# Gating and squares moved into a scan, diagonal matmuls for scaled transposes, and a first modulation in two halves

## The reference

```python
mod = silu(cond) @ w_mod + b_mod                      # six rows of 1024, two conditionings
h = rmsnorm(x + pos, norm1_w) * (1 + sc1) + sh1       # pos: a 2-D grid of sines, latent tokens only
gate_a, gate_b, u, v, z, xbc, dt_f, dt_b = split(h @ w_in)
y_f, h_f = ssd_chunked(xh, dt_f, ...)                 # 32 heads of 64, chunks of 128 tokens, state 128
y_r, h_b = ssd_chunked(flipped, ...)
y = y_f + flip(y_r) + xh * d_skip                     # 640 x 2048
y = group_rmsnorm(y * silu(z), ssd_norm_w, 4 groups)  # mean of squares over 512 columns
merged = sigmoid(gate_a) * (y_a @ w_branch_a) + sigmoid(gate_b) * (y @ w_branch_b)
x = x + g1 * (merged @ w_out)                         # then a routed mixture of experts
```

## Time and profile before

| | us |
|---|---|
| median of 3 runs | 1561.56 (1560.65 to 1561.61) |
| the profiled execution | 1557.0 |
| its span, first to last instruction | 1555.3 |

### The profile page before, as it was taken

How to read it: one execution, slowest core, us unless ns; L and a number is a source line. 1 busy time by engine, 2 the same in 40 slices (tenths; PEclk the granted TensorE clock), 3 DMA queues, 4 the chain that set the end, 5 groups by cost and what they waited for, 6 DMA issues and landing times. The chain is left out here.

```text
span 1555.3 us, 20614 instructions
## 1 busy us (share of the span) xinstructions
PE 1302.7 (84%) x7887; PEld 1154.1 (74%) x7887; DVE 835.1 (54%) x972; ACT 668.5 (43%) x1031; POOL 263.5 (17%) x285
## 2 busy tenths in 40 slices
PE   3999989799998999947788844999880799999970
PEld 1789989799997888944566643999770688888860
DVE  2411442277665111105778759333464499999966
ACT  2423330144443222127567737111140477777743
POOL 0600000000000010025599861000002000000002
PEclk9999999999999999978899966999985899999995
DMA  9992112112212243154466541331645599999935
GB/s 385 412 363 71 66 38 99 37 55 82 70 67 82 90 148 123 52 185 142 149 190 196 199 153 78 115 107 64 259 162 194 195 397 405 421 403 413 413 154 203
DMA packets 62497, 289.09 MB, mean 186 GB/s; under 512 B 9104, under 2 KB 13648, under 8 KB 42064
## 3 DMA queue, kind: packets, MB, share of 16 engines
q1 hardware_dynamic: 49424, 242.19, 42.0%
q0 software_dynamic: 12608, 45.62, 7.5%
q10 hardware_dynamic: 384, 0.16, 0.0%
HBM read 239.51 MB, written 48.43 MB: 185 GB/s over the span
## 5 line engine op out<-in xcount | busy, mean ns | idle before, releaser
L212 PE MATMUL banks<-rounded,rounded 128*128 128x320 f32 (+1 forms) x1168 | 366.1, 313 | 20.2 <-DVE rounded L735 6.9
L213 PE MATMUL banks<-rounded,rounded 128*128 128x320 f32 (+1 forms) x1168 | 363.9, 312 | 0.0
L214 PE MATMUL banks<-rounded,rounded 128*128 128x320 f32 (+1 forms) x1168 | 363.7, 311 | 0.0
L191 DVE TENSOR_TENSOR rounded<-words,rounded 128x2048 fp32r<-128x2048 f32 x52 | 119.2, 2292 | 225.7 <-ACT rounded L183 223.4
L1916 DVE TENSOR_TENSOR rounded<-words,rounded 128x2048 fp32r<-128x2048 f32 x96 | 219.7, 2290 | 32.9 <-ACT rounded L1907 32.0
L212 PEld LDWEIGHTS banks<-rounded,rounded 128*128 128x128 f32 (+1 forms) x1168 | 220.8, 189 | 21.5 <-issue 13.9
L213 PEld LDWEIGHTS banks<-rounded,rounded 128*128 128x128 f32 (+1 forms) x1168 | 220.9, 189 | 0.3
L214 PEld LDWEIGHTS banks<-rounded,rounded 128*128 128x128 f32 (+1 forms) x1168 | 220.6, 189 | 0.3
L1907 ACT ACTIVATE rounded<-words 128x2048 fp32r<-128x2048 f32 x96 | 183.9, 1916 | 47.1 <-PE banks L2032 39.4
L183 ACT ACTIVATE rounded<-words 128x2048 fp32r<-128x2048 f32 x52 | 99.3, 1909 | 138.0 <-PE banks L233 62.8
L1191 ACT ACTIVATE words<-words,words 128x128 f32<-128x128 f32 x320 | 97.7, 388 | 62.0 <-DMA words<-decay_sums 62.0
(11 more groups left out here) (269 smaller groups left out, 1971.7 us busy)
## 6 DMA issues: line engine op xcount, KB each, us to landing
words<-in_units SPq DMA_DIRECT2D x52, 1024.0 KB, 5.0
words<-in_wg SPq DMA_DIRECT2D x32, 1024.0 KB, 7.4
words<-in_wu SPq DMA_DIRECT2D x32, 1024.0 KB, 7.7
words<-in_wd SPq DMA_DIRECT2D x32, 1024.0 KB, 8.2
words<-decay_sums SPq DMA_DIRECT2D x40, 512.0 KB, 3.8
words<-in_w_mod_rest SPq DMA_DIRECT2D x32, 512.0 KB, 4.3
slot_rows<-words POOLq DMA_DIRECT2D x27, 512.0 KB, 24.1
expert_rows<-words POOLq DMA_DIRECT2D x25, 512.0 KB, 9.1
```

Of the source, the lines that this page charges most:

```text
L191: self.nc.vector.tensor_tensor(self.lo[:, i % 2, :], self.raw[:, i % 2, :], self.hi[:, i % 2, :].bitcast(F32), ALU.subtract).then_inc(self ...
L212: nc.tensor.matmul(out, lhs[0](k), rhs[0](k), start=(k == 0), stop=False)
L213: nc.tensor.matmul(out, lhs[0](k), rhs[1](k), start=False, stop=False)
L214: last = nc.tensor.matmul(out, lhs[1](k), rhs[0](k), start=False, stop=(k == nk - 1))
```

## The change

Three things are done, and a number of small ones follow from them.

- **First modulation in two halves.** The weight pieces 0 and 2 (first half of shift and of scale) are loaded first, then weight unit 0, then pieces 1 and 3, then unit 1. Two small vectors move ahead of x. The sums and columns of the first half (three of now six `s_cols`) release the first four slices; the second half's products stand in TensorE's list between the second and third tile, its sums after the third tile. The position table becomes a row table and a column table, spread by the transfer. A root on an unused element is done at the start. The zeros, the constants and the further weight units wait for the sixth `s_cols`.
- **Gating, squares and roots in the scan.** For 18 of the 20 (chunk, group) pairs, SP loads silu(z) (256 KB, one slot), GpSimd multiplies (`apply_z`, at even sub-steps), ScalarE squares (`squares`, at odd sub-steps from 7) into the same slot. Mean, reciprocal and root of the first 16 are done at the scan's end.
- **Diagonal transposes.** In the normalization GpSimd writes `ident` times the reciprocal root as a diagonal for each pair, and TensorE multiplies the block of y with it, in place of a scaling and a transpose. ScalarE and VectorE split 512 elements at once. The norm weight goes onto the weight units of branch b: GpSimd scales each of eight units (`scale`) before it is split.

The diff, cut to what matters:

```diff
+O_SQ = O_TMP + 4192
+O_NW = O_K + 848
+GROUPS = [(c, g) for c in (0, 4, 3, 2, 1) for g in range(G)]
+GATED, ROOTED = 18, 16
...
+    def scale(self, pool, i, column):
         i += self.first
-        act.wait_ge(self.raw_loaded[i % 2], 16 * (i // 2 + 1))
+        pool.wait_ge(self.raw_loaded[i % 2], 16 * (i // 2 + 1))
+        v = self.raw[:, i % 2, :].rearrange("p (k n) -> p k n", k=KI)
+        self.nc.gpsimd.tensor_tensor(v, v, column.unsqueeze(2).broadcast_to([P, KI, UNIT // KI]),
+                                     ALU.mult).then_inc(self.scaled, 1)
+    def split_hi(self, act, i, scaled=False):
+        i += self.first
+        if scaled:
+            act.wait_ge(self.scaled, i + 1)
+        else:
+            act.wait_ge(self.raw_loaded[i % 2], 16 * (i // 2 + 1))
...
-    WM = [kit.at(o, 4096) for o in (O_H, O_H + 5120, O_MG, O_BC + 2304)]
-    RB = (4, 5, 7, 3)
+    WM = [kit.at(o, 4096) for o in (O_H, O_MG, O_H + 5120, O_BC + 2304)]
+    RB, SB = (4, 0, 7, 1), ((6, 0), (2, 384))
     x = kit.at(O_X, NC, D)
-    pos = kit.at(O_X + 5120, NC - 1, D)
+    pos_row, pos_col = kit.at(O_X + 5120, NC - 1, 512), kit.at(O_X + 7168, 512)
...
-            sp.dma_start(x, io["x"].rearrange("(c p) d -> p c d", p=P)).then_inc(s_x, 16)
-            sp.dma_start(pos, io["pos"].rearrange("(c p) d -> p c d", p=P)).then_inc(s_pos, 16)
-            sp.dma_start(kit.at(O_K, KOFF["end"]), io["consts"]).then_inc(s_k, 16)
             sp.dma_start(n1, io["norm1"]).then_inc(s_small, 16)
             sp.dma_start(bcol, io["b_mod_cols"].rearrange("p (q k) -> p q k", q=2)).then_inc(s_small, 16)
-            for j in range(4):
+            sp.dma_start(x, io["x"].rearrange("(c p) d -> p c d", p=P)).then_inc(s_x, 16)
+            sp.dma_start(pos_col, io["pos_col"]).then_inc(s_pos, 16)
+            for h in range(2):
+                sp.dma_start(pos_row[64 * h:64 * h + 64].rearrange("p c d -> p (c d)"),
+                             io["pos_row"][h:h + 1].partition_broadcast(64)).then_inc(s_pos, 16)
+            sp.dma_start(kit.at(O_K, KOFF["end"]), io["consts"]).then_inc(s_k, 16)
+            for j in (0, 2):
                 sp.dma_start(WM[j], io["w_mod"][j]).then_inc(s_w[j], 16)
             w.load(sp, 0)
+            for j in (1, 3):
+                sp.dma_start(WM[j], io["w_mod"][j]).then_inc(s_w[j], 16)
             w.load(sp, 1)
-            sp.wait_ge(s_dve, 2)
+            sp.wait_ge(s_dve, 4)
             sp.dma_start(scr["xp"].rearrange("(c p) d -> p c d", p=P), x).then_inc(s_xp, 16)
-            sp.wait_ge(s_sum, 1)
-            sp.wait_ge(s_cols, 3)
+            sp.wait_ge(s_sum, 2)
+            sp.wait_ge(s_cols, 6)
...
-            pool.wait_ge(s_cols, 3)
+            pool.wait_ge(s_cols, 6)
...
+            def modulate(half):
+                for j in (half, 2 + half):
+                    pe.wait_ge(s_w[j], 16)
+                    for k in range(KD):
+                        g = k % 4
+                        last = nc.tensor.matmul(ps[32 * g:32 * g + 32, RB[j], :], sc[:, k, :], WM[j][:, k * 512:(k + 1) * 512],
+                                                start=(k < 4), stop=(k >= 4))
+                    last.then_inc(s_row, 1)
+            def add_parts(half):
+                bank, at = SB[half]
+                for n, j in enumerate((half, 2 + half)):
+                    pe.wait_ge(s_part, 2 * half + n + 1)
+                    for q in range(4 * j, 4 * j + 4):
+                        last = nc.tensor.matmul(ps[:, bank, at + 2 * q:at + 2 * q + 2], row[:, q * P:(q + 1) * P], sel, start=True, stop=True)
+                last.then_inc(s_sum, 1)
...
+            modulate(0)
+            add_parts(0)
+            pe.wait_ge(s_dve, 6 + NC)
...
+                if k in (0, 4):
                     turn(k // 2 + 1)
+                if k == 1:
+                    pe.wait_ge(s_full, 8)
+                    modulate(1)
+                if k == 2:
+                    add_parts(1)
+                    pe.wait_ge(s_cols, 6)
+                    turn(2)
...
+            nc.scalar.activation(unused, sc[:, 0, 31:32], ACT.Sqrt).then_inc(s_table, 1)
...
+            copy_rows(0)
             w.split_hi(act, 0)
             for k in range(KD):
+                if k == 4:
+                    copy_rows(1)
+                    w.split_hi(act, 1)
...
+            columns(0)
             w.split_lo(dve, 0)
             for k in range(KD):
+                if k == 4:
+                    columns(1)
+                    w.split_lo(dve, 1)
...
+            def load_z(i):
+                if i:
+                    sp.wait_ge(squared, i)
+                c, g = GROUPS[i]
+                sp.dma_start(Z, scr["z"][c * P:(c + 1) * P, cols(g)]).then_inc(z_loaded, 16)
...
+                if j >= 3 and j % 2 and (j - 1) // 2 < GATED:
+                    load_z((j - 1) // 2)
...
+            def apply_z(i):
+                c, g = GROUPS[i]
+                if c:
+                    pool.wait_ge(y_whole, 2 * i + 2 - N0)
+                else:
+                    pool.wait_ge(y_steps, 2 * i + 2)
+                pool.wait_ge(z_loaded, 16 * (i + 1))
+                nc.gpsimd.tensor_tensor(X[:, c, cols(g)], X[:, c, cols(g)], Z, ALU.mult).then_inc(z_applied, 1)
...
+                if j and j % 2 == 0 and j // 2 <= GATED:
+                    apply_z(j // 2 - 1)
...
+            def squares(i):
+                c, g = GROUPS[i]
+                act.wait_ge(z_applied, i + 1)
+                nc.scalar.activation(Z, X[:, c, cols(g)], ACT.Square, accum_out=ssq[:, i:i + 1]).then_inc(squared, 1)
             for j, (c, g, q) in enumerate(subs):
+                if j >= 7 and j % 2:
+                    squares((j - 7) // 2)
...
+            squares(GATED - 1)
+            act.wait_ge(mean_done, 2)
+            nc.scalar.activation(rr[:, 0:ROOTED], rr[:, 0:ROOTED], ACT.Sqrt).then_inc(root_done, 1)
...
+            dve.wait_ge(squared, ROOTED)
+            nc.vector.tensor_scalar(ssq[:, 0:ROOTED], ssq[:, 0:ROOTED], 1.0 / GW, EPS, ALU.mult, ALU.add).then_inc(mean_done, 1)
+            dve.wait_ge(mean_done, 1)
+            nc.vector.reciprocal(rr[:, 0:ROOTED], ssq[:, 0:ROOTED]).then_inc(mean_done, 1)
...
+    early, late = kit.at(O_TMP + 2560, 12, P), kit.at(O_NW + KI, 8, P)
+    diag = lambda i: early[:, i, :] if i < 12 else late[:, i - 12, :]
...
+            for i in range(GATED, n):
+                c, g = GROUPS[i]
+                sp.dma_start(Z[:, i - GATED, :], scr["z"][tokens(c), cols(g)]).then_inc(s_z[i - GATED], 16)
+            sp.dma_start(nw, io["ssd_nw"]).then_inc(s_in, 16)
...
+            def scales(i):
+                nc.gpsimd.tensor_tensor(diag(i), ident, rr[:, i:i + 1].broadcast_to([P, P]), ALU.mult).then_inc(s_diag, 1)
+            for i in range(ROOTED):
+                scales(i)
+            for i in range(GATED, n):
+                c, g = GROUPS[i]
+                pool.wait_ge(s_z[i - GATED], 16)
+                nc.gpsimd.tensor_tensor(X[:, c, cols(g)], X[:, c, cols(g)], Z[:, i - GATED, :], ALU.mult).then_inc(s_y, 1)
+            pool.wait_ge(s_in, 16)
+            w.scale(pool, 0, nw)
+            pool.wait_ge(s_root, 1)
+            for i in range(ROOTED, n):
+                scales(i)
...
+            for i, (c, g) in enumerate(GROUPS):
+                pe.wait_ge(s_diag, i + 1)
+                if i >= 8:
+                    pe.wait_ge(s_lo, i - 7)
+                for q in range(4):
+                    k = 4 * g + q
+                    last = nc.tensor.matmul(ps[:, i % 8, q * P:(q + 1) * P], X[:, c, k * P:(k + 1) * P], diag(i), start=True, stop=True)
+                last.then_inc(s_tr, 1)
...
+            for i, (c, g) in enumerate(GROUPS):
+                act.wait_ge(s_tr, i + 1)
+                nc.scalar.activation(hi[:, 4 * g:4 * g + 4, tokens(c)], turned(i), ACT.Copy).then_inc(s_hi, 1)
+                if i == 7:
+                    for k in range(GATED, n):
+                        m, h = GROUPS[k]
+                        act.wait_ge(s_y, k - GATED + 1)
+                        nc.scalar.activation(Z[:, k - GATED, :], X[:, m, cols(h)], ACT.Square, accum_out=ssq[:, k:k + 1]).then_inc(s_sq, 1)
+                if i == 9:
+                    act.wait_ge(s_ms, 2)
+                    nc.scalar.activation(rr[:, rest], rr[:, rest], ACT.Sqrt).then_inc(s_root, 1)
+            w.split_hi(act, 0, scaled=True)
...
+            for i, (c, g) in enumerate(GROUPS):
+                dve.wait_ge(s_hi, i + 1)
+                at = lo[:, 4 * g:4 * g + 4, tokens(c)]
+                nc.vector.tensor_tensor(at, turned(i), hi[:, 4 * g:4 * g + 4, tokens(c)].bitcast(F32), ALU.subtract).then_inc(s_lo, 1)
+                if i == 7:
+                    dve.wait_ge(s_sq, n - GATED)
+                    nc.vector.tensor_scalar(ssq[:, rest], ssq[:, rest], 1.0 / GW, EPS, ALU.mult, ALU.add).then_inc(s_ms, 1)
+                    dve.wait_ge(s_ms, 1)
```

(21 more changed lines are left out.)

155 lines of the change are left out of this document (44 added, 111 removed).

## The result

| | median us (runs) | ratio to before, 95% interval | profiled execution, span |
|---|---|---|---|
| before | 1559.73 (11) | | 1557.0, 1555.3 |
| after | 1550.66 (11; 1542.27 to 1558.69) | 0.9949 [0.9932, 0.9966] | 1542.27, 1540.6 |

The change makes the kernel faster by 0.5%, some 8 us (0.0051 x 1559.73). The sign was right, the size was not: 27 us were forecast, the medians are 9 apart, and 1550.66 lies above the range. The profiled execution of after is the fastest of its eleven, so its trace shows 14.7 of gain (1557.0 - 1542.27), not 8. Both gaps need an explanation: 1529.8 to 1542.3 in the profile, and 1542.3 to 1550.7 beside it.

A forecast was written before the change was run, and what follows sets the result against it. Bounds: feeding TensorE in the opening, GpSimd in the scan's middle, a chain with no full engine in the normalization. 1557.0 - 3.6 + 10.4 - 34 = 1529.8 profiled, 4.6 more for the median: 1534.4; range 1525 to 1549.

The forecast's parts named there:

- opening: Start to the eight tiles' end: first tile 10.1 us earlier, 6.5 added inside the tiles, net -3.6; bounds -6 to -1.
- scan: Products, squares and z loads added to the scan cost +10.4 us, mostly on GpSimd; bounds +3 to +30.
- normalization: Barrier to next stage: diagonal products replace scalings and transposes, -34 us; bounds -21 (clock stays low) to -36.
- branch b and later: Branch b: GpSimd's seven unit scalings, 4.6 us each, hide under TensorE's products; uncovered they would cost 4.6 once.
- eleven products at 1.00, two of the three hidden: 9: Scan, sub-steps 10 to 30: GpSimd products at 1.00 us each, two of three beside waits hide, 9 us.
- no new meeting: Scan: the new GpSimd product adds no further overlap with VectorE's decay product (one costs 0.98 us), so 1.00 is charged.
- SP's standing at the z load: Scan: SP stands until 8.0 of a pair, modulation pieces up to 3.2 us late; taken as 0, range 0 to 8.
- The last chunk: End of the scan: three GpSimd products, two of them beside waits, cost 1 us.
- Chunk 0: Scan's first chunk: four products fall where GpSimd waits 16.6 us for VectorE, cost 0.
- the low-clock rival: Normalization: TensorE stays at 1.2 GHz, 13 us more, time 1547; chance 0.10.
- the lock costs both engines: Scan: products meet VectorE and lengthen decay products; fifteen at 2.02, scan +30, time 1554, half 1544; chance 0.14.
- The circle of the z slot: Scan, SP between square and load: GpSimd waits for z, pairs of 12.9, 51 us, time 1575; chance 0.04.

The follow-up runs named there:

- no_product: The changed kernel without the 18 products of silu(z) and y in the scan (z still loaded, y squared ungated): 1544.80 us, 0.9905 of before.
- free_z: The changed kernel with the square's unused result in its own place, so the next z load waits for the product alone: 1544.36 us, 0.9905 of before.
- after_again: The changed kernel unaltered, run for a second profile: median 1549.94 us, 0.9948 of before; profiled execution 1542.23 us.
- z_by_act: The changed kernel with z loads issued by ScalarE right behind its own square instead of by SP, still one slot: 1546.91 us, 0.9910 of before.
- dve_free_z: free_z with the 18 products on VectorE, one pair behind, instead of GpSimd: 1546.63 us, 0.9920 of before.
- half_dve: free_z with every second product behind chunk 0 (seven of 14) on VectorE: 1542.74 us, 0.9878 of before.
- dve_shift: free_z with all 18 products on VectorE, two sub-steps behind the group's end, z loads and squares one pair later: 1539.28 us, 0.9883 of before.
- the two kernels with twelve groups: free_z and dve_shift, each with twelve groups gated in the scan and eight in the normalization: 1541.38 and 1535.98 us, 0.9898 and 0.9863 of before.
- old_opening_free_z: free_z with the opening of the kernel before (modulation and position table whole): 1547.99 us, 0.9908 of before.

## Why the prediction was wrong

Terms in us; measured in the two profiles. The opening is read at the end of the eight tiles, the scan from sub-step 0 to 39, the normalization from there to branch b, the rest to the end of the span.

| term | forecast | measured |
|---|---|---|
| opening | -3.6 | -2.1 (77.83 to 75.75) |
| scan | +10.4 | +19.7 (208.5 to 228.2) |
| normalization | -34 | -35.4 (66.4 to 31.0) |
| branch b and later | 0 | +2.9 (580.9 to 583.9) |
| sum (with 0.1 between tiles and scan) | -27.2 | -14.7 |

The prediction drew the line between scan and normalization at the barrier. Read so, the scan took 16.8 more (215.0 to 231.9, from sub-step 0 to its last instruction), since its end behind sub-step 39 got 2.8 shorter (6.5 to 3.7), and the normalization 32.5 less (59.8 to 27.3).

- **The scan is the step that failed**, and in it the line "eleven products at 1.00, two of the three hidden: 9". They cost 15.3 (122.8 - 107.5). The product's price was too low: 1.27 long and 1.24 to the next start, not 1.04 and 1.00, so 14.0 us of GpSimd's time and not 11. I had taken the row of a product whose second operand is broadcast (L1014); a product of two whole operands stood in the view as well, 4.58 for 2,048 elements, which is 1.15 for 512. And "no new meeting" was not nothing: GpSimd's other lines took 3.2 longer in sum (117.45 - 100.27 less 14.0). What hid was as forecast: GpSimd's idle time fell by 1.9 (7.3 to 5.4). 14.0 + 3.2 - 1.9 = 15.3, in place of 11 - 2 = 9. This is read from one profile; in the second the pairs cost 18.2 (125.7 - 107.5).
- **SP's standing at the z load, which I put at 0,** was the second failure, hidden by the first. I had SP standing until 8.0 of a pair and a weight piece "up to 3.2 us late", and let TensorE's 1 us of slack a pair cover it. The delay was right (TensorE's waits reach 3.2 in no_product), the cover was not: by itself it costs about 13 in the 11 pairs (120.1 - 107.5) and 7 in the last chunk. In after it costs little in the profile, since GpSimd's longer pairs cover it (123.2 in free_z without it, 122.8 with it).
- **The last chunk** was put at 1 and cost 4.3 in after's profile, but 1.1 in after_again's. In the first GpSimd waits there for z (L1092) in three places, 5.0 us in all; with the z load freed the chunk takes 30.7, as before. That points to the z slot again.
- **Chunk 0** was put at 0: +0.1 in after. In free_z, z_by_act, dve_free_z, half_dve and dve_shift it took 5 to 7 more, in the two kernels with twelve groups 2.5 to 2.9, in old_opening_free_z 1.5; why is open.
- **The opening** brought 1.5 less than forecast: the second weight piece came 1.9 late, and the tiles took 0.4 less than reckoned.
- **The normalization** came out close to what was worked out: 27.3 from the barrier where 26.1 was reckoned. TensorE's first product came 2.0 behind the scan's last instruction and not 0.4, since GpSimd's first diagonal had to be written; the products took 20.1 (19.7 reckoned) and the tail 5.2 (6). The last four diagonals were written by 945.2 (943.76 + 1.48), and TensorE, which had 160 products until 951.5, did not wait for them; its granted clock was 0.50 until 935 and 1.00 from 936, as assumed. The bound of -21 for a clock that stays low does not come out of its own terms: 914.9 + 34 + 6 = 954.9 is -19.5.
- **Branch b**: the seven scalings hide, as forecast (GpSimd 26.24 us, TensorE never waits). Of the 2.9 us, 1.1 lie in branch b, whose first 6.2 us go at a granted clock of 0.50 (1.2 GHz), where 3.6 did before. The next stage too starts longer at the lower clock (last section), but has all but 0.4 of that back 85 us later; the other 1.4 lie behind that and are not explained.
- **The rivals.** By number alone the profile falls on the low-clock rival (1547 less 4.6 is 1542.4) and the median between it and the full form of "the lock costs both engines" (1554). That is chance: neither is in the trace as it was put. TensorE reached 1.00 in the normalization. The new products took 1.27 at the median and 1.72 at most, not 2.02; and VectorE's decay product, which was to lengthen, got shorter on the mean over the 11 pairs, as its lines in after and in before show (the second profile has 1619 ns):

```profile
L1357 DVE TENSOR_TENSOR words<-words,words 128x1024 f32<-128x1024 f32 x22 | 33.8, 1535 | 0.0
```

```profile
L1279 DVE TENSOR_TENSOR words<-words,words 128x1024 f32<-128x1024 f32 x22 | 36.9, 1679 | 0.0
```

  The circle of the z slot decides nothing at this pair length, as argued (pairs of 11.2, under 12.0), but its place, SP between square and load, was where the second price sat.
- **The median** stands 8.4 above the profiled execution where I carried over 4.6 from before. The profiled executions are the two fastest of 17. With the z load freed, five runs lie within 1.3 us around their profile; but old_opening_free_z, with the same SP order in the scan, spreads by 7.8. After's three slowest runs (1557.08 to 1558.69) have mean granted clocks of 0.914 to 0.918, the profiled one 0.924; but 1550.79 has 0.924 too. Whether the clock lengthens them or drops because TensorE waits is not settled.

By the Trainium skill, GPSIMD Engine Reference, section 4.1 Engine selection, elementwise products belong on VectorE, which is about twice as fast. For this product the shortest durations agree (1.262 on GpSimd in after, 0.679 on VectorE in dve_shift, a ratio of 1.86); the mean on VectorE in the middle of the scan, 1.275, does not. The move was worth 0.6 us a pair, not 1.27.

## What to carry to other kernels

When a stage is held by one engine, ask what would hold it next, and price an added edit on both: here GpSimd's product and SP's late weight pieces cost nearly the same, and either experiment alone would have "shown" that its part costs the pairs next to nothing. A load that waits for a slot in an issuing queue delays everything that is queued behind it (weight pieces by up to 3.2 us here); give the slot's release to the earliest reader (here by a scratch place for an output nobody reads). And take an instruction's price from a row with the same kind of operands, not of the same size alone.

## What the runs showed of the hardware

- GpSimd's products of 512 elements take 1.04 at the least with a broadcast operand (L1071) and 1.26 at the least with two whole ones (L1092); of 2,048 elements 3.63 (L188) and 4.58. I had priced the weight scaling at 4.6.
- VectorE's product of two whole 128x512 operands ranges from 0.68 to 1.46: in dve_shift's timeline 0.68 in the four places where no GpSimd instruction overlaps it, 1.45 to 1.46 in the eight where it begins 0.13 us behind the start of a GpSimd instruction of 1.04. The lines of after and of dve_shift:

```profile
L1092 POOL TENSOR_TENSOR words<-words,words x18: 1262/1272/1717, 719.7 to 918.4; 128x512 f32<-128x512 f32 x18
```

```profile
L1001 DVE TENSOR_TENSOR words<-words,words x18: 679/1055/1464, 739.4 to 922.3; 128x512 f32<-128x512 f32 x18
```

- Two waits of the same length left TensorE at different clocks. Behind branch b it stood still for 4.03 us before the change (to 1092.90) and 4.04 after it (to 1076.40); the windows of 4 us that take in the end of the wait have a granted clock of 0.75 in before and 0.50 in after (before, then after):

```profile
1092.00:1096.00 4.00, 3.10 (x10) 2.46 (x11) 1.48 (x2) 1.92 (x1) 0.93 (x4) 0.75 0.50 131
```

```profile
1076.00:1080.00 4.00, 3.60 (x9) 2.85 (x10) 1.77 (x1) 1.91 (x1) 0.94 (x4) 0.50 0.66 187
```

So the length of a wait alone did not tell what the next stage's start costs; here its first 58 us, up to TensorE's next wait of over 0.8 us, took 1.1 longer in after (59.4 against 58.3).
